# Odd layer's attention: the streams' forgetting bias as 24 bf16 rows added by TensorE, in place of 128 full fp32 rows read from HBM

## The reference, cut to what matters

```python
fq = jnp.cumsum(logf, axis=1)
c_after = lax.cumsum(clogf, axis=1, reverse=True) - clogf
fk = jnp.concatenate([-c_after, fq], axis=1)
kk = jnp.concatenate([ck, k], axis=1)                 # 1024 cached keys and the 16 own ones
s = jnp.einsum('bihd,bjhd->bhij', q, kk) * (D ** -0.5)
s = s + fq.transpose(0, 2, 1)[..., :, None] - fk.transpose(0, 2, 1)[..., None, :]
s = jnp.where(valid, s, -jnp.inf)
p = jax.nn.softmax(s, axis=-1)
return jnp.einsum('bhij,bjhd->bihd', p, vv)
```

## Time and profile before

| | us |
|---|---|
| median of 3 runs (2692.27 to 2693.68) | 2693.63 |
| the profiled execution's own time | 2691.87 |
| its span | 2690.0 |
| TensorE matmuls busy | 2550.0 (95%) |
| DVE busy | 1637.6 (61%) |
| ACT busy | 955.5 (36%) |
| GpSimd busy | 785.3 (29%) |

### The profile page before, as it was taken

One profiled execution on the slowest core, in us unless ns is written; L12 is line 12 of the kernel. 1 busy time (PEld: TensorE's weight loads), 2 busy tenths in 40 slices (PEclk: granted clock), 3 DMA queues, 4 the chain that ended last, 5 costly groups with the idle time before them and its releaser, 6 DMA issues.

```text
span 2690.0 us, 45814 instructions
## 1 busy us (share of the span) xinstructions
PE 2550.0 (95%) x18803; PEld 2409.7 (90%) x18803; DVE 1637.6 (61%) x2438; ACT 955.5 (36%) x1493; POOL 785.3 (29%) x434
## 2 busy tenths in 40 slices
PE   7999999999789999999899999999888898999997
PEld 7999999998659999999899999999844488999997
DVE  7777587222446968488877758721133349685675
ACT  5333242220264424243433324221055444243341
POOL 1322323331151232323232332332133341323232
PEclk8999999999699999999999999999989999999998
DMA  3222222222361222222222222225699931222221
GB/s 112 71 87 87 87 71 88 79 69 108 114 228 48 69 89 86 88 79 73 70 67 91 86 83 76 88 98 145 226 356 370 366 139 48 80 86 79 87 79 71
DMA packets 79223, 304.16 MB, mean 113 GB/s; under 512 B 10769, under 2 KB 18722, under 8 KB 64050
## 3 DMA queue, kind: packets, MB, share of 16 engines
q1 hardware_dynamic: 79026, 301.39, 33.0%
HBM read 279.95 MB, written 21.41 MB: 112 GB/s over the span
## 4 chain that ended last, share of the span: by engine, by line
PE 79%; DVE 9%; DMA 5%; issue 3%; ACT 2%; POOL 1%; DVEq 0%; SPq 0%; ACTq 0%; POOLq 0%
PE ps L382 34%; PE ps L869 33%; PE ps L1258 4%; DMA kv_ring<-in_fox_kc 4%; DMA kv_ring<-in_fox_vc 1%; PE ps L1580 1%; PE ps L1614 1%; DVE wb_lo L706 1%; PE ps L1539 1%; PE ps L1554 1%; DVE gate_prod L1076 1%; POOL w_lo L368 1%; PE ps L1595 1%; DVE w_raw L672 1%; PE ps L1565 1%
## 5 line engine op out<-in xcount | busy, mean ns | idle before, releaser
L869 PE MATMUL ps<-xs_hi,wb_hi 128*128 128x320 f32 x2112 | 659.6, 312 | 24.1 <-POOL wb_lo L755 12.7
L869 PE MATMUL ps<-xs_hi,wb_lo 128*128 128x320 f32 x2112 | 655.7, 310 | 0.0
L869 PE MATMUL ps<-xs_lo,wb_hi 128*128 128x320 f32 x2112 | 655.5, 310 | 0.0
L368 POOL TENSOR_TENSOR w_lo<-w_raw,w_hi 128x1024 fp32r<-128x1024 f32 (+2 forms) x130 | 398.6, 3067 | 612.7 <-ACT w_hi L364 612.7
L755 POOL TENSOR_TENSOR wb_lo<-w_raw,wb_hi 128x512 fp32r<-128x512 f32 x176 | 268.7, 1531 | 962.1 <-PE ps L869 777.4
L869 PEld LDWEIGHTS ps<-xs_hi,wb_hi 128*128 128x128 f32 x2112 | 399.3, 189 | 28.0 <-POOL wb_lo L755 13.4
L869 PEld LDWEIGHTS ps<-xs_lo,wb_hi 128*128 128x128 f32 x2112 | 399.5, 189 | 1.0 <-issue 1.0
L869 PEld LDWEIGHTS ps<-xs_hi,wb_lo 128*128 128x128 f32 x2112 | 399.3, 189 | 0.0
L364 ACT ACTIVATE w_hi<-w_raw 128x1024 fp32r<-128x1024 f32 (+2 forms) x130 | 158.3, 1217 | 647.7 <-PE ps L382 511.5
L382 PE MATMUL ps<-h_hi,w_hi 128*128 128x320 f32 x1408 | 322.1, 310 | 3.4 <-DVE h_lo L1070 3.4
L382 PE MATMUL ps<-h_hi,w_lo 128*128 128x320 f32 x1408 | 320.8, 309 | 0.0
(11 more groups left out here) (242 smaller groups left out, 4312.6 us busy)
## 6 DMA issues: line engine op xcount, KB each, us to landing
w_raw<-in_w_up SPq DMA_DIRECT2D x175, 512.0 KB, 4.4
kv_ring<-in_fox_kc SPq DMA_DIRECT2D x32, 1024.0 KB, 13.4
kv_ring<-in_fox_vc SPq DMA_DIRECT2D x32, 1024.0 KB, 13.0
w_raw<-in_w_down_a SPq DMA_DIRECT2D x64, 384.0 KB, 3.1
w_raw<-in_w_in SPq DMA_DIRECT2D x24, 1024.0 KB, 4.8
w_raw<-in_w_down_b SPq DMA_DIRECT2D x32, 512.0 KB, 3.5
fox_s_s<-s_bias_dram SPq DMA_DIRECT2D x16, 576.0 KB, 10.0
kv_ring<-in_band_kc SPq DMA_DIRECT2D x8, 1024.0 KB, 6.9
```

Source lines behind the costliest of these rows:

```text
L368: nc.gpsimd.tensor_tensor(out=w_lo[:, slot, 0:cols], in0=w_raw[:, slot, 0:cols], in1=w_hi[:, slot, 0:cols].bitcast(F32), op=ALU.subtract). ...
L869: last = nc.tensor.matmul(ps[:, bank, 0:HALF], w_part[:, slot, cols], x_part[:, k, :], start=k == 0 and i == 0, stop=k == 3 and i == 2)
```

## The change

The bias is kept as one row for each stream and head. DVE splits it into three bf16 parts (the value rounded to bf16, the rest rounded, the rest of that) after `c_after` is copied. Two stores put the parts into HBM: 128 x 3 x 1024 bf16 and 16 x 3 x 128. Each unit loads 3 x 8 rows of 1024 bf16 (three loads of 16 KB, one of each part); the own keys' rows are loaded once. TensorE adds them to the logits in PSUM by a product with a constant `row_heads`, whose 24 rows hold 0 and 1 and give each of the 128 rows its head; its three parts are made by three loads at the program's start that read a 128 x 8 constant turned. DVE's instruction for the maximum stays as it is but reads a column of zeros in place of the bias tile.

```diff
@@ constants and tiles
+    zero = const("zero", [P, 1])
+    row_heads = const("row_heads", [P, P], BF16)
+    fox_tiles["s_rows"] = [place(f"bias_rows{u}", [24, PAST], BF16, at_rows[u]) for u in range(2)]
+    fox_tiles["own_rows"] = place("own_bias_rows", [24, 2, P], BF16, at_rows[1] + PAST * 2)
+    c_parts = place("c_parts", [P, 3, PAST], BF16, at_e)
+    own_parts = place("own_parts", [H_C, 3, P], BF16, at_e + 3 * PAST * 2)
@@ cast_masks (DVE, first SwiGLU, behind its first group)
+        nc.vector.memset(zero[:, :], 0.0).then_inc(masks_cast, 1)
+        dve.wait_ge(row_heads_loaded, 48)
+        nc.vector.tensor_copy(row_heads[0:24, :], row_heads_f[0:24, :]).then_inc(masks_cast, 1)
@@ load_sample_bias (SP)
+            if self.masked:
+                if n == 0:
+                    for part in range(3):
+                        sp.dma_start(self.tiles["own_rows"][8 * part:8 * part + 8, :, :], ...
+                                     ).then_inc(self.own_loaded, 16)
+                else:
+                    if n >= 2:
+                        sp.wait_ge(self.slogits_ready, n - 1)
+                for part in range(3):
+                    sp.dma_start(self.tiles["s_rows"][n % 2][8 * part:8 * part + 8, :],
+                                 s_rows_dram[part, 8 * n:8 * n + 8, :]).then_inc(self.sbias_loaded[n % 2], 16)
+                return
@@ s_logits (TensorE)
                 for ch in range(self.chunks):
+                    if self.masked:
+                        if ch == 0:
+                            pe.wait_ge(self.sbias_loaded[n % 2], 48 * (n // 2 + 1))
+                        nc.tensor.matmul(ps[:, 4 + ch, 0:512], row_heads[0:24, :],
+                                         self.tiles["s_rows"][n % 2][:, 512 * ch:512 * ch + 512], start=True, stop=False)
                     pe.wait_ge(self.ring_loaded[r], loaded)
                     for p in range(4):
                         last = nc.tensor.matmul(ps[32 * p:32 * p + 32, 4 + ch, 0:512], qz_s[:, n % 2, p, :],
-                                                kv_ring[r][:, p, :], start=True, stop=True)
+                                                kv_ring[r][:, p, :], start=not self.masked, stop=True)
@@ behind the causal mask of the own keys
+                    nc.tensor.matmul(ps[:, bank, 0:P], row_heads[0:24, :], self.tiles["own_rows"][:, g, :],
+                                     start=False, stop=False)
@@ s_maxes (DVE)
-                dve.wait_ge(self.sbias_loaded[u], 16 * (n // 2 + 1))
+                elif n >= 2:
+                    dve.wait_ge(self.spt_ready, len(self.parts) * (n - 1))
+                bias = zero[:, :].broadcast_to([P, cols]) if self.masked else s_s[u][:, 0:cols]
@@ fgate_dve, behind the copy of c_after
+            for rest, parts in ((neg_f[:, SEQ:], own_parts), (c_after[:, :], c_parts)):
+                for part in range(3):
+                    if part:
+                        dve.wait_ge(f_parts, done)
+                        nc.vector.tensor_tensor(out=rest, in0=rest, in1=parts[:, part - 1, :],
+                                                op=ALU.subtract).then_inc(f_parts, 1)
+                        done += 1
+                        dve.wait_ge(f_parts, done)
+                    nc.vector.tensor_copy(parts[:, part, :], rest).then_inc(f_parts, 1)
+                    done += 1
@@ SP, at the start, behind the constants
+            for part in range(3):
+                sp.dma_start(row_heads_f[8 * part:8 * part + 8, :], ins["own_rows"].rearrange("t b -> b t")
+                             ).then_inc(row_heads_loaded, 16)
@@ SP, odd mixer, behind the store of p_bias_dram
-                for b in range(DEC_BATCH):
-                    sp.dma_start(s_bias_dram[b * H_C:(b + 1) * H_C, :, PAST:], ...).then_inc(f_scratch, 16)
-                sp.dma_start(s_bias_dram[:, 0:half, 0:PAST], repeated).then_inc(f_scratch, 16)
+                sp.wait_ge(f_parts, 10)
+                sp.dma_start(own_rows_dram.rearrange("p h c -> h p c"), own_parts[:, :, :]).then_inc(f_scratch, 16)
+                sp.dma_start(s_rows_dram.rearrange("p r c -> r p c"), c_parts[:, :, :]).then_inc(f_scratch, 16)
                 sp.dma_start(outs["fox_logf"], lf[:, :]).then_inc(logf_stored, 16)
                 load_slabs(sp, ph, "in", 10, 2, m["fm"][0] + 10)
-                sp.dma_start(s_bias_dram[:, half:, 0:PAST], repeated).then_inc(f_scratch, 16)
```

More of the change, by code:

```diff
@@ L142, in trunk_program @@
     own_head = const("own_head", [P, 2])
+    zero = const("zero", [P, 1])
+    row_heads = const("row_heads", [P, P], BF16)
+    row_heads_f = place("row_heads_f", [P, P], F32, at_ffh[0] + 15 * T * 4 + P * 4 + 240 * 4)
     neg_max = const("neg_max", [P, 8])
@@ L223, in trunk_program @@
     fox_tiles = attention_tiles("fox", at_dead, at_g, PAST + P)
+    at_rows = (at_g + 10752, (at_dead + 16384 + (PAST + P) * 4 + 63) // 64 * 64)
+    fox_tiles["s_rows"] = [place(f"bias_rows{u}", [24, PAST], BF16, at_rows[u]) for u in range(2)]
+    fox_tiles["own_rows"] = place("own_bias_rows", [24, 2, P], BF16, at_rows[1] + PAST * 2)
+    assert at_rows[0] + PAST * 2 <= at_c and at_rows[1] + PAST * 2 + 4 * P <= end
     qc = place("qc", [P, KT, T], F32, at_hid[1])
@@ L279, in trunk_program @@
     y_stored, masks_cast = sem("y_stored"), sem("masks_cast")
+    row_heads_loaded = sem("row_heads_loaded")
     plain_hi, sum_hi, plain_lo, sum_lo, sum_done = (
@@ L1081, in ffn_dve @@
             if ph["index"] == 0 and g_ == 1:
-                dve.wait_ge(masks_cast, 3)
+                dve.wait_ge(masks_cast, 7)
             for t in range(lo, hi):
@@ L1424, in __init__ @@
             self.ring_loaded = [s(f"ring_loaded{r}") for r in range(RING)]
-            self.sbias_loaded = two("sbias_loaded")
+            self.sbias_loaded, self.own_loaded = two("sbias_loaded"), s("own_loaded")
             self.sqz_done, self.slogits_ready, self.smax_step = s("sqz_done"), s("slogits_ready"), s("smax_step")
@@ L1732, in s_maxes @@
                 cols, u = self.cached + P, n % 2
-                dve.wait_ge(self.sbias_loaded[u], 16 * (n // 2 + 1))
+                if not self.masked:
+                    dve.wait_ge(self.sbias_loaded[u], 16 * (n // 2 + 1))
+                elif n >= 2:
+                    dve.wait_ge(self.spt_ready, len(self.parts) * (n - 1))
                 dve.wait_ge(self.slogits_ready, n + 1)
+                bias = zero[:, :].broadcast_to([P, cols]) if self.masked else s_s[u][:, 0:cols]
                 nc.vector.memset(s_marks[:, u:u + 1], 0.0)
-                nc.vector.tensor_tensor_reduce(out=s_s[u][:, 0:cols], in0=s_s[u][:, 0:cols], in1=flat(4, 3, cols),
+                nc.vector.tensor_tensor_reduce(out=s_s[u][:, 0:cols], in0=bias, in1=flat(4, 3, cols),
                                                scale=-1.0, scalar=-LOWEST, op0=ALU.add, op1=ALU.min,
@@ L2176, in _ @@
             sp.dma_start(dst[tuple(slice(None) for _ in dst.shape)], ins[name]).then_inc(consts_loaded, 16)
+        with nc.allow_non_contiguous_dma("128 x 8 of 0 and 1"):
+            for part in range(3):
+                sp.dma_start(row_heads_f[8 * part:8 * part + 8, :], ins["own_rows"].rearrange("t b -> b t")
+                             ).then_inc(row_heads_loaded, 16)
         for ph in PLAN:
```

28 lines of the change are left out of this document (15 added, 13 removed).

## The result

The changed kernel takes 2677.93 us (median of 3 runs, 2671.14 to 2678.31), 15.7 us less than before, ratio 0.9937 with an interval of 0.992 to 0.9954. The forecast was 2675.8 us.

What follows compares the result with a forecast made beforehand. It took DMA transfers to bound the odd attention, TensorE next. (28.44 - 25.7) x 6.5 = 17.8 us saved gave 2674.1 us for the profiled execution, 2675.8 as median; own range 2671 to 2681, 8-in-10 range 2666 to 2690.

Steps and rivals of the forecast that it cites:

- The limit before: Odd attention: DMA transfers set the pace, 0.99 busy, 28.44 us an iteration of two units; TensorE is the next limit.
- The tile at 1.63 us: Odd attention's DMA queue: each bias tile load of 0.590 MB that falls away is worth 1.63 us.
- 25.4 us as the transfers' floor: Odd attention: without tiles an iteration carries 9.01 MB, which at 355 GB/s takes 25.4 us.
- The 0.3 us for interplay: Odd attention: added to 25.4 us an iteration because some chunk waits remain, bounds 0 and 1.0, giving 25.7.
- The signs that I had named: Right: keys every 25 to 26 us, DMA share above 0.95; wrong: share under 0.9 with iterations of 24.4 us.
- TensorE's floor: Odd attention: TensorE alone needs 23.1 us an iteration, plus 1.27 for the new products: 24.4 us.
- How many iterations gain: Odd attention: 13 of 15 tile loads lie on the path, so 6.5 iterations gain 28.44 - 25.7 us each.
- Transfers gain more than their bytes: Rival, odd attention: bias tiles cause the rate dips, so TensorE's 24.4 us limits; 28 us saved, 2665.6; chance 0.12.
- TensorE takes the place of the DMA: Rival, odd attention: products at low clock behind the chunks' landing, iteration 27.0 us; 9.4 us saved, 2684.3; chance 0.12.
- No gain: Rival, odd attention: the loop from key issue to landing, not bytes, keeps 28.4 us an iteration; 2693.6; chance 0.05.
- Each small load holds the queue: Rival, odd attention: 45 loads of 16 KB hold the queue 0.7 us each; 7.0 us slower, 2700.6; chance 0.05.
- The edits at nothing: Moved waits, DVE's split (7.1 us), fewer stores and the turned loads at the start (16.2 us of cover) cost nothing.

Runs made afterwards that it cites:

- e7: The kernel before with the change's three products a unit added on TensorE, rows of zeros, tiles still loaded: 2694.91 us, ratio 1.0006.
- e2: The kernel before with the bias tile loaded for the first two units only, no products added: 2671.72 us, ratio 0.9925.
- e10: The kernel before with only half of each bias tile loaded from the third unit on: 2682.24 us, ratio 0.9959.
- e3: The changed kernel without its three bias products on TensorE, rows still loaded and waited for: 2675.43 us, ratio 0.9943.
- e4: The changed kernel with SP's wait ahead of the rows put back behind the unit's transposes: 2677.91 us, ratio 0.9958.
- e5: The changed kernel with one load of 32 rows a unit in place of three loads of 8: 2682.15 us, ratio 0.9959.
- e6: The changed kernel with a unit's three bias products side by side ahead of its keys: 2676.77 us, ratio 0.9943.
- e1: The changed kernel measured again, no edit, in more runs: 2678.34 us, ratio 0.9953.
- e8: The kernel before with only the three turned loads at the start, their cast and the column of zeros, unused: 2694.10 us, ratio 1.0006.
- e12: The changed kernel with the edits of e11 and e6 together: 2666.88 us, ratio 0.9905.
- e11: The changed kernel with the prompt's bias read from 64 copies in HBM instead of 8: 2672.78 us, ratio 0.9930.

## Why the prediction came out

**The limit before: right, and shown.** e7 shows that TensorE was not it, e2 and e10 that bytes were. The tile at 1.63 us is confirmed as far as profiles can tell: 3.2 us a pair against 3.26.

**25.4 us as the transfers' floor: the size is about right, a floor it is not.** Where the transfers hold the pace, an iteration takes what I said: 25.7 us in e3, with TensorE's work taken away, and 25.4 to 25.8 in e4, e5 and e6. But the kernel after moved the same 9.01 MB in 24.43 us, six times in a row, at 367 and 368 GB/s and a DMA share of 0.93, and e1 did so four times. The 355 GB/s that I divided by was what the queue gave in five iterations of the kernel before, not what it can give; over the last iteration before 2154.64 us that kernel itself had 414 GB/s, with keys, values and a tile in the queue and no prompt bias:

```profile
2130.10:2154.64 24.54, 22.16 (x299) 12.95 (x302) 9.55 (x45) 13.34 (x36) 8.40 (x9) 1.00 1.01 414
```

The 0.3 us for interplay can't be told from the spread.

**The signs that I had named** were mostly missed, and one of those for *wrong* came true: an iteration of 24.4 us with TensorE as the limit, at a DMA share of 0.93 in it and 0.89 over the attention. Of those for *right*, the share is not above 0.95, the waits for keys and values are 5.1 and in e1 7.0 us instead of 10 to 15, the clock is 1.00 in the steady iterations and 0.94 over the attention, and the new products take 0.32 us and not 0.24. No wait for `s_rows` is named and slab 1 is in time, as forecast. "What is late next is still the keys" holds for e3 to e6 and for the end of e1, and not for the execution that the forecast was for.

**TensorE's floor: the sum right by luck, both terms wrong.** I had 23.1 + 1.27 = 24.4 us, and 24.43 is what it is. But the long products are 0.32 us, not 0.237. Three of them with their change of weights make 0.80 us a unit by the chain, and the keys' two products, which ran as one group of 1.85 us, now take 2 x 0.99. With that a unit grew from 1.85 + 0.16 to 2.94 us, 1.86 an iteration where I had 1.27. The rest is then 24.43 - 1.86 = 22.6, not 23.1. Of that difference 0.1 is my reading of the second half of the 1.85 us, whose first instruction starts at 2154.64 and not at 2154.75. The term of the dense run of the earlier trace rows was mis-sized because it is a price inside a row of equal products; here each new product stands alone between others. e6 shows the same products as a group: two in 0.44 us.

```profile
2057.94 0.60 PE L1607 MATMUL ps<-bias_rows,row_heads 24*128 24x512 bf16 x2
2058.38 0.21 PE L1609 MATMUL ps<-own_bias_rows,row_heads 24*128 24x128 bf16 x1
2058.52 1.06 PE L1615 MATMUL ps<-kv_ring,fox_qz_s 128*32 128x512 f32 x8
```

**How many iterations gain.** I took 6.5 at 2.74 us. The 28.44 is the mean of five distances in the middle; over all seven the kernel before has 27.84. My 25.7 was as much too high, so the two errors cancel in the difference. In the kernel after the first distance is 27.60 us, part of it at the low clock, and no better than before; then six at 24.43. Over seven distances it is 7 x (27.84 - 24.88) = 20.7 us, of which the attention keeps 18.8; in e1 7 x (27.84 - 25.16) = 18.8 and 17.0. 17.8 lies between; that it fits so well is in part these errors cancelling.

**The rivals.** *Transfers gain more than their bytes* named the right end, 24.4 us with TensorE as the limit, and it is what the profiled execution does in its steady state. Its cause is refuted: e2 keeps the dips. Its price was too high, since the first iteration gives nothing and not every execution gets there. What I had put against it, that the prompt's biases can make the dips as well, is borne out by where the dips lie and by the copies. *TensorE takes the place of the DMA* fell with the clock: 1.00 in the steady iterations. *No gain* fell with the landing at 8.5 us: the 13.5 had been queue. *Each small load holds the queue*: not seen at 0.7 us a load, as e5 is no faster with a third of them; the Trainium skill's figures for loads under 64 KB (page "DMA: Bandwidth & Descriptors", section "Bandwidth"), which would make the kernel 6 us slower, don't add up like that here, by the time; the page took them from loads that GpSimd issues, and these are SP's. By the rule of the same page on the 8 engines, section "Why a DMA increments its semaphore by 16 and not by 1", a load of 32 rows should have given back 0.27 us an iteration, less 0.09 for its zeros, an estimate of 1.2 us in all; e5 has an interval of 0.9946 to 0.9972, 7 us wide, and neither bears that out nor refutes it. That the three loads go over 8 engines and the one over 16, the trace agrees: 9 and 16 updates, as told above. I had overlooked that the prompt's biases, whose source has 8 copies as its first dimension, are such loads too.

**The edits at nothing.** The split on DVE, for the earlier trace rows:

```profile
1848.08 0.21 DVE L2201 CAST own_parts<-neg_f 16x128 bf16<-16x128 f32 x1
...
1849.35 0.67 DVE L2201 CAST c_parts<-c_after 128x1024 bf16<-128x1024 f32 x1
1850.06 1.23 DVE L2197 TENSOR_TENSOR c_after<-c_after,c_parts 128x1024 f32<-128x1024 f32 x1
...
1853.30 0.70 DVE L2201 CAST c_parts<-c_after 128x1024 bf16<-128x1024 f32 x1
1853.91 0.82 DVE L1362 SCALAR_TENSOR_TENSOR kc<-ps,inv_rms 128x640 f32<-128x640 f32 x1
```

It takes 5.9 us, not 7.1, because a cast to bf16 of 1024 columns is 0.67 to 0.70 us and not 1.22; the eviction is not late. The start, for the earlier trace rows:

```profile
12.47 4.93 SPq L2230 DMA_DIRECT2D row_heads_f<-in_own_rows  x3
17.45 1.37 SPq L343 DMA_DIRECT2D w_raw<-in_w_up  x1
18.85 0.43 SPq L345 DMA_DIRECT2D w_raw<-in_w_up  x1
```

The turned loads hold SP itself, 1.6 us each, and slab 1's second load goes out 5.7 us later; it is used at 33.57 us where it was 33.78. The cover held. It was smaller than I had said: the 4.4 us to landing in the earlier trace rows are those of slab 1's other line of loads, L333; the one issued at 13.17 landed 6.2 us later, at 19.4 and not 17.6, which leaves 14.4 us.

**Outside 1938 to 2175 us.** I had said that a gain or loss there would mean that I looked in the wrong place. The first profile shows 4.5 us of gain ahead and 2.5 of loss behind. e1 takes the gain back. The loss is there in e7 (518.4 us), e2 (518.5), e10 (518.4) and e8 (517.3) as well, whose code behind the attention is the kernel before's; so the 515.3 of the one profile of before is more likely the exception. Together they leave the place right.

**The whole.** The attention gave 17.0 to 18.8 us in profiles against the one of before, 15.3 to 17.1 against e8, and the timed runs 12.5 and 15.7. The forecast of 17.8 us is at the upper end of what was found. The rest of the difference is within the spread.

## What to carry to other kernels

Work out for the stretch how long one iteration needs on each resource alone, not only on the one that bounds it: here 28.4 by transfers stood over 22.6 by TensorE, and the change moved work from the first to the second until both stood near 25. When two limits have met, relieving one shows little and relieving both shows more than the two apart: from 0.9953 (e1) the copies alone reach 0.9930, the grouped products alone 0.9943, both 0.9905. A rate read off one busy stretch is not yet a limit: ask in which stretch the same queue moves more, and what it loads there. And what an added product costs has to be read where it will stand; alone between others it cost 0.32 us, in a group 0.22.

## What the runs showed of the hardware

- Storing a row that 128 partitions read 64 times in HBM instead of 8 made a transfer-bound stretch faster: the lowest slices rose from 207 to 253 up to 299 to 349 GB/s (e6, e12) and from 176 to 239 up to 235 to 280 (kernel after, e11), at the same bytes loaded. It was worth 10 us of 2677 (e6 to e12). The loads left 9 updates on their semaphore with 8 copies and 16 with 64, so the number of DMA engines changed together with the number of readers, and the runs don't divide the two.
- While such loads from 8 copies run, the 8 KB pieces of keys and values beside them take 468 ns (median, e6), and 314 ns from 64 copies (e12).
- The same 9.01 MB an iteration went through at 367 to 368 GB/s in one execution and at about 350 in others (e3, e4, e5: 25.7 to 25.8 us).
- A load that reads its source turned, 1024 elements of 4 bytes, holds SP for 1.6 us where most loads of constants beside it take 0.4.
- A bf16 product of 24 rows and 512 columns costs 0.32 us between products with other weights and 0.22 beside its like, at a granted clock of 1.00.
- The clock column counts as 1.00 what lies ahead of the first entry of the clock's record (22.5 us in the kernel before, 35.1 in the one after). The spacing of equal matmuls, 0.27 or 0.14 us for 320 columns, tells the level there.
